# Opening of a two-layer transformer trunk: x loaded in two column halves, one mask made earlier

## The chip, the cores and the metric

One NeuronCore of a Trainium2 chip runs the whole program in one launch. The metric is the device time of that launch in microseconds (us). TensorE (PE) does matmuls and transposes, VectorE (DVE) and ScalarE (ACT) elementwise work, GpSimd (POOL) a few selects and rotary products, SyncE (SP) issues nearly all transfers from HBM (DMA).

## The reference, cut to what matters

```python
for l in range(2):
    h = rms_norm(x, norm1_g[l])                    # x: 256 tokens x 1024, float32
    z = h @ w_in[l] + b_in[l]                      # 1024 x 8448, cut into q/k/v, gMLP, dilated q/k/v, gates
    oa = sliding_window_attention(...)             # window 128, sinks, partial rotary
    ob = spatial_gating(...)                       # tril(w_spatial) inside chunks of 128
    oc = dilated attention, (window, dilation) in ((128, 1), (512, 4), (2048, 16))
    x = x + (sum of gated projections) @ w_out[l]
    x = x + hier_moe(rms_norm(x, norm2_g[l]), ...) # 32 experts
return rms_norm(x, norm_f_g)
```

## The kernel before, in words

Tokens lie on the 128 partitions in two blocks (`TB = 2`), so x is a tile `xs` of 128 x 2 x 1024. For `h @ w_in` the contraction must lie on partitions: x is turned on PE into 8 blocks of 128 columns (`KB = 8`), four of them per pair of PSUM banks. Each float32 product is made of three fp32r passes (high x high, low x high, high x low): ACT writes the rounded high part of a weight piece (`whi`, line 868) and of x (`ahi`, line 853), DVE the rest (`wlo`, line 1058; `alo`, line 1045). The gain of the norm goes in with `ahi` and `alo`; the norm's 1/rms comes in later, when a result leaves PSUM (`z_out`, line 1077).

The unit of the trunk is a half item, numbered j: two 128-row blocks of `w_in` by 512 columns, cast by one `whi` instruction and two `wlo` instructions (called here high(j), and low(j) with its first and second half), used by 12 matmuls of 512 columns on PE, called conv(j): `first_conv` for j = 0 to 3 in layer 0 and 1, `z_conv` afterwards. `whi` and `wlo` have two buffers, so high(j) waits until conv(j-2) is done. Weights come through a ring of four slots; a slot holds two half items.

The engines run written-out streams side by side and meet at semaphores. The opening in layer 0, by engine:

- SP issues x as one transfer (line 682), the first ring slot in two halves (line 679, for j = 0 and j = 1), three more slots (line 673), a broadcast of `b_in` (line 695), `w_spatial` (line 696), then slots as they come free; after four of these it waits for `masks_made` and stores the masks to DRAM (line 713), since their room is needed later.
- ACT issues the gains and the positions, loads a table, waits for `gains_done`, then does `x_high` (two blocks of x), high(0), `x_high`, high(1), four blocks of `x_high`, high(2), and so on; after high(3) it squares x for the norm (line 874).
- POOL makes index tiles and the identity; later it waits for `w_spatial` and masks its upper triangle (line 792).
- DVE makes the mask of branch A and the dilated mask 0 (lines 396, 399), waits for the turned gains and copies them (line 413), then follows ACT. A dilated mask with a step over 1 takes four instructions (lines 404, 405, 406, 399); masks 1 and 2 are made after low(4) and after low(7). After low(5) it evacuates the first results (line 1077), after low(6) it makes the rotary angles (`rope_angles`).
- PE runs `WARM_SETUP` = 7 float32 products of the identity with itself (two records each, line 1351), turns the gains (line 1355), waits for x and turns all 8 blocks (16 transposes, line 1363), then runs conv(0) on. Before conv(6) it turns `w_spatial` (line 1417).

Of the kernel before, what the change touches and what calls it, by code (L numbers as in the profile page):

```python
# [77 lines left out]
def trunk_program(nc, x, positions, norm1_g, w_in, b_in, attn_sinks, sgu_ln_g, sgu_ln_b, w_spatial,  # L78
# [7 lines left out]
    with ExitStack() as whole:  # L86
# [141 lines left out]
        y_low = sem("y_low")  # L228
        final_in = sem("final_in")
        masks_made = sem("masks_made")  # L230
        masks_out = sem("masks_out")
        masks_in = sem("masks_in")
        x_in = sem("x_in")
        pos_in = sem("pos_in")
        gain_in = sem("gain_in")
        gain2_in = sem("gain2_in")
# [111 lines left out]
            for _ in range(n):  # L348
                pe.matmul(ps[:, bank, 0:2 * P], ident[:], wr[:].rearrange("p k n -> p (k n)")[:, 0:2 * P], start=True, stop=True)

        WARM_SETUP, WARM_ROUTE, WARM_RANKS, WARM_LAST = 7, 7, 1, 1

        def load_sqrt_table(act):
            act.activation(warm[:], warm[:], ACT.Sqrt)
# [32 lines left out]
        def setup_dve(dve, link):  # L387
            dve.memset(warm[:], 1.0).then_inc(warm_set, 1)
            dve.wait_ge(consts_ready, 1)
            link(dve.tensor_copy(dist[:], dist_i[:]))  # L390
            link(dve.tensor_scalar(causal[:], dist[:], 0.0, None, ALU.is_ge))

            def make_mask(m, win, valid):

                if win < S - 1:
                    link(dve.scalar_tensor_tensor(out=within[:], in0=dist[:], scalar=float(win),
                                                  in1=valid[:], op0=ALU.is_le, op1=ALU.mult))
                    valid = within
                link(dve.tensor_scalar(m, valid[:], 1.0, -NEG, ALU.subtract, ALU.mult))

            def make_dilated(g, win, dil):

                if dil > 1:
                    link(dve.tensor_scalar(rem_i[:], dist_i[:], dil - 1, None, ALU.bitwise_and))
                    link(dve.tensor_copy(rem[:], rem_i[:]))
                    link(dve.scalar_tensor_tensor(out=rem[:], in0=rem[:], scalar=0.0, in1=causal[:],
                                                  op0=ALU.is_equal, op1=ALU.mult))
                make_mask(mask_c[:, g, :], win, rem if dil > 1 else causal)

            make_mask(mask_a[:], A_WIN - 1, causal)  # L410
            make_dilated(0, *C_PAIRS[0])
            dve.wait_ge(gains_ready, 1)
            dve.tensor_copy(gains[:, 0:DEPTH * KB], ps[:, 0, 0:DEPTH * KB]).then_inc(gains_done, 1)
            return make_dilated

        def rope_angles(dve, link):
# [172 lines left out]
        def trunk_stage(l):  # L589
            with ExitStack():  # L590
# [75 lines left out]
                with ExitStack():  # L666
                    @block.sync
                    def _(sp):
# [3 lines left out]
                            dst = ring[:, s, :].rearrange("p (k n) -> p k n", k=4)  # L672
                            sp.dma_start(dst, src).then_inc(ring_in[s], 16)

                        def load_first_item():
                            dst = ring[:, 0, :].rearrange("p (k n) -> p k n", k=4)
                            for half, landed in ((0, first_in), (1, ring_in[0])):
                                ks = slice(2 * half, 2 * half + 2)
                                sp.dma_start(dst[:, ks, :], w_in_l[:, ks, 0:BANK]).then_inc(landed, 16)

                        if l == 0:
                            sp.dma_start(xs[:], x.rearrange("o (t p) d -> p (o t) d", p=P)).then_inc(x_in, 16)
                        else:
                            sp.wait_ge(before_me.gu_ready, QUADS - 1)
                        load_first_item()
                        if l:
                            sp.wait_ge(before_me.y_ready, 2 * (QUADS - 1))
                            sp.wait_ge(before_me.st_ready, QUADS)
# [18 lines left out]
                        if l:  # L707
                            sp.wait_ge(before_me.gu_ready, QUADS)
                            sp.wait_ge(before_me.y_ready, 2 * QUADS)
                            sp.dma_start(masks, mask_store).then_inc(masks_in, 16)  # L710
                        else:
                            sp.wait_ge(masks_made, 1)
                            sp.dma_start(mask_store, masks).then_inc(masks_out, 16)
                        sp.dma_start(ln_gb[:, 0, :], sgu_ln_g[l].partition_broadcast(P)).then_inc(ln_in, 16)
                        sp.dma_start(ln_gb[:, 1, :], sgu_ln_b[l].partition_broadcast(P)).then_inc(ln_in, 16)
                        with sp.Fori(2, CHUNKS // 2) as it:
# [13 lines left out]
                        for i, (w, r) in enumerate(proj):  # L730
                            item = 34 + i
                            sp.wait_ge(low_split, 2 * (item - 4 + 1))
                            if w in ("a", "b", "out"):
                                dst = ring[:, item % 4, :].rearrange("p (k n) -> p k n", k=4)
                                for w_half, kb, n, nh, at in halved_blocks(w, r):
                                    src = w_half[kb * P:(kb + n) * P, nh * BANK:(nh + 1) * BANK].rearrange("(k p) n -> p k n", p=P)
                                    sp.dma_start(dst[:, at:at + n, :], src).then_inc(ring_in[item % 4], 16)
                            else:
                                src = w[2 * r * P:2 * (r + 1) * P, :].rearrange("(k p) n -> p k n", p=P)
                                dst = ring[:, item % 4, :].rearrange("p (k n) -> p k n", k=2)  # L740
                                sp.dma_start(dst, src).then_inc(ring_in[item % 4], 16)

                            if item == 35:
                                with nc.allow_non_contiguous_dma(reason="small parameters"):
                                    sp.dma_start(gain2[:], norm2_g[l].rearrange("(p k) -> p k", k=KB)).then_inc(ahead_in, 16)
                                    for w_r, first, n in ((w_router_group, 0, GROUPS), (w_router_expert, GROUPS, EXPERTS)):
                                        sp.dma_start(wr[:, :, first:first + n],
                                                     w_r[l].rearrange("(k p) n -> p k n", p=P)).then_inc(ahead_in, 16)
                            if item == 37:  # L750
                                sp.wait_ge(s_free, BATCHES)
                                if l == 0:
                                    sp.wait_ge(masks_out, 16)
                                load_last_down(sp, l, 3)
                            if item == 38:
                                sp.wait_ge(sv_ready, 1)
                                sp.wait_ge(pv_mm, turned_before(BATCHES))
                                load_ahead(18, 19)
                            if item == 39:
                                sp.wait_ge(obt_ready, 3)  # L760
                                sp.wait_ge(o_lo, 5)
                                load_ahead(0, 1, 5)
                            if item == 42:
                                sp.wait_ge(gated, 4)
                                load_ahead(2, 6)
                            if item == 43:
                                sp.wait_ge(gated, 8)
                                load_ahead(4)
# [268 lines left out]
                    def _(dve):  # L1037
# [43 lines left out]
                        for j in range(8):  # L1081
# [8 lines left out]
                            if l == 0 and j == 2:  # L1090
                                dve.wait_ge(gains_ready, 2)
                                dve.tensor_copy(gains[:, DEPTH * KB:], ps[:, 2, 0:DEPTH * KB]).then_inc(gains_done, 1)
                            if l == 0 and j in (4, 7):
                                make_dilated(1 if j == 4 else 2, *C_PAIRS[1 if j == 4 else 2])
                                if j == 7:
                                    dve.sem_inc(masks_made, 1)
                            if l and j == 2:
                                for q in range(4):
                                    dve.wait_ge(before_me.back_ready, 4 * (QUADS - 1) + q + 1)
# [114 lines left out]
                        low_at(43)  # L1214
                        dve.wait_ge(small_in, 32)
                        if l:
                            dve.wait_ge(masks_in, 16)
                        softmax_in(0)
                        low_at(44)
                        z_out(4, AHEAD - 1, BANK, AHEAD)  # L1220
# [125 lines left out]
                    def _(pe):  # L1346

                        if l == 0:
# [4 lines left out]
                            def turn_gains(i, bank):  # L1353
                                rows = DEPTH * KB
                                pe.transpose(ps[:, bank, 0:rows], gain_rows[:, i, :], ident[0:rows, 0:rows]).then_inc(gains_ready, 1)

                            pe.wait_ge(gain_in, 16)
                            turn_gains(0, 0)
                            pe.wait_ge(x_in, 16)
                            for k in range(KB):  # L1360
                                for tb in range(TB):
                                    at = (k % 2) * S + tb * P
                                    mm = pe.transpose(ps[:, 4 + k // 2, at:at + P], xs[:, tb, k * P:(k + 1) * P], ident[:])
                                if k % 2:
                                    mm.then_inc(turned, 1)
                            pe.wait_ge(gain2_in, 16)
                            turn_gains(1, 2)
                            pe.wait_ge(gains_done, 1)
# [52 lines left out]
                        for j in range(8):  # L1421
# [5 lines left out]
                            if j == 6:  # L1427
                                if l:
                                    pe.wait_ge(before_me.back_done, 4 * QUADS)
                                turn_w_spatial()  # L1430
                            if j < 4:
                                first_conv(j)
                            else:
# [946 lines left out]
```

## Time and profile before

| what | value |
|---|---|
| device time, 3 runs | median 1040.52 us (1038.24 to 1041.02) |
| profiled execution | 1039.62 us, span 1037.9 us |
| granted TensorE clock, mean over the span | 0.975 |
| PE / DVE / ACT / POOL busy | 956.8 / 576.1 / 426.5 / 58.5 us |
| DMA | 313.04 MB, mean 302 GB/s |

The span is what the profile covers, from the first instruction; the device time is some 1.7 us more. Busy time is a share over stages with different limits, so what matters for the change is the order of events in the first 40 us. A row of the timeline or the chain gives the start in us, the length in us, the engine, the line of the kernel and what it writes and reads; "x16" means 16 records merged.

### The profile page before, as it was taken

The page shows a single profiled execution, that of the slowest core. Times are in us where ns is not written, and L with a number is a line of the kernel's source. Part 1 is how long each engine was busy: PE and PEld are TensorE (multiplying, and loading weights), DVE is VectorE, ACT ScalarE, POOL GpSimd, SP SyncE. Part 2 cuts the span into 40 slices and gives each one's busy share as a digit, 9 for nine tenths or more (in the row PEclk, how much of TensorE's full clock was granted, in tenths as well). Part 3 has the DMA queues.
Part 4 walks back from the last instruction along what each step waited for, and adds up shares of the span by engine and source line. Part 5 has one row for each costly group of instructions (what it writes and reads, how often), then busy time and mean ns, then how long its engine had stood idle before and what let it go on. Part 6 is the DMA issues. An engine that isn't in the chain of part 4 may idle for free.

```text
span 1037.9 us, 15396 instructions
## 1 busy us (share of the span) xinstructions
PE 956.8 (92%) x5894; PEld 665.7 (64%) x5894; DVE 576.1 (56%) x1186; ACT 426.5 (41%) x907; POOL 58.5 (6%) x74
## 2 busy tenths in 40 slices
PE   8999999999999996795999999999999999875796
PEld 7788877777887432542588887777788954332343
DVE  7766788886873331121176668898869533222212
ACT  5434566666443210110354355666664431111122
POOL 1120400000010000000004004000000100000000
PEclk9999999999999997898999999999999999998889
DMA  9965533247999999999998655332589999999996
GB/s 347 357 222 186 198 123 122 82 122 260 397 360 381 418 426 424 420 423 427 414 380 278 202 187 177 122 122 82 167 291 369 381 402 417 426 422 424 425 424 255
DMA packets 97114, 313.04 MB, mean 302 GB/s; under 512 B 13424, under 2 KB 18576, under 8 KB 74512
## 3 DMA queue, kind: packets, MB, share of 16 engines
q1 hardware_dynamic: 96704, 312.04, 79.2%
q8 instruction: 45, 0.74, 0.3%
q14 instruction: 29, 0.24, 0.1%
q10 hardware_dynamic: 336, 0.02, 0.0%
HBM read 310.20 MB, written 1.84 MB: 301 GB/s over the span
## 4 chain that ended last, share of the span: by engine, by line
PE 67%; DMA 13%; DVE 7%; SPq 6%; ACT 3%; issue 2%; DVEq 0%; POOLq 0%; ACTq 0%
PE ps L1374 14%; PE ps L1376 13%; PE ps L1375 13%; DMA arena<-in_w_expert_up_dram 8%; SPq L479 6%; PE ps L1974 5%; DMA ring_rest<-in_w_expert_up_dram 5%; PE ps L2038 2%; PE ps L1949 2%; PE ps L1494 2%; PE ps L1399 2%; PE ps L1502 2%; DVE wlo L1058 2%; PE ps L2050 1%; PE ps L1922 1%
## 5 line engine op out<-in xcount | busy, mean ns | idle before, releaser
L1374 PE MATMUL ps<-whi,ahi 128*128 128x512 f32 (+1 forms) x736 | 285.0, 387 | 4.4 <-DVE wlo L1058 3.7
L1058 DVE TENSOR_TENSOR wlo<-arena,whi 128x512 fp32r<-128x512 f32 (+1 forms) x352 | 234.2, 704 | 91.3 <-ACT whi L868 88.8
L1376 PE MATMUL ps<-whi,alo 128*128 128x512 f32 (+1 forms) x736 | 277.1, 376 | 0.0
L1375 PE MATMUL ps<-wlo,ahi 128*128 128x512 f32 (+1 forms) x736 | 276.8, 376 | 0.0
L868 ACT CAST whi<-arena 128x1024 fp32r<-128x1024 f32 (+1 forms) x176 | 180.6, 1028 | 184.6 <-PE ps L1376 177.9
L1374 PEld LDWEIGHTS ps<-whi,ahi 128*128 128x128 f32 x736 | 138.5, 188 | 35.5 <-DVE wlo L1058 8.4
L1376 PEld LDWEIGHTS ps<-whi,alo 128*128 128x128 f32 x736 | 138.4, 188 | 26.0
L1375 PEld LDWEIGHTS ps<-wlo,ahi 128*128 128x128 f32 x736 | 138.7, 188 | 23.1
L1974 PE MATMUL ps<-arena,rows 128*32 128x512 f32 x416 | 92.1, 628 | 15.1 <-DMA arena<-in_w_expert_up_dram 11.6
L1974 PE MATMUL ps<-ring_rest,rows 128*32 128x512 f32 x352 | 78.0, 643 | 20.0 <-DMA arena<-in_w_expert_up_dram 17.0
L2166 DVE SCALAR_TENSOR_TENSOR acts<-ps,wslot,acts 128x256 f32<-128x256 f32 x16 | 7.7, 483 | 155.9 <-ACT acts L1884 132.8
L1884 ACT ACTIVATE acts<-ps,rslot 128x256 f32<-128x256 f32 x16 | 7.6, 474 | 156.2 <-PE ps L1974 153.3
L1949 PE MATMUL ps<-arena,work 128*128 128x128 f32 x448 | 55.5, 283 | 13.9 <-DVE arena L2125 12.2
L1949 PEld LDWEIGHTS ps<-arena,work 128*128 128x128 f32 x448 | 52.8, 197 | 24.0 <-DVE arena L2125 13.8
L948 ACT ACTIVATE probs<-probs,neg 128x128 f32<-128x128 f32 x112 | 49.5, 444 | 32.7 <-DVE neg L1183 32.7
L2050 PE MATMUL ps<-rows,st 128*128 128x512 f32 x112 | 54.9, 612 | 0.2
L2038 PE MATMUL ps<-arena,acts 128*32 128x512 f32 x288 | 48.1, 664 | 6.9 <-ACT acts L1888 4.9
L1974 PEld LDWEIGHTS ps<-ring_rest,rows 128*32 128x32 f32 x352 | 20.8, 117 | 52.4 <-issue 52.4
L1974 PEld LDWEIGHTS ps<-arena,rows 128*32 128x32 f32 x416 | 24.3, 115 | 44.6 <-issue 44.6
L2150 DVE TENSOR_TENSOR xs<-ps,xs 128x512 f32<-128x512 f32 x56 | 38.7, 691 | 22.7 <-PE ps L2050 22.7
L1077 DVE SCALAR_TENSOR_TENSOR arena<-ps,rstd,arena 128x512 f32<-128x512 f32 (+2 forms) x68 | 46.6, 726 | 2.2 <-PE ps L1376 2.2
L2142 DVE TENSOR_SCALAR rows<-ps,gain 128x128 f32<-128x128 f32 x56 | 15.8, 343 | 40.4 <-PE ps L1949 40.4
(282 smaller groups left out, 1043.2 us busy)
## 6 DMA issues: line engine op xcount, KB each, us to landing
arena<-in_w_in_dram SPq DMA_DIRECT2D x62, 1024.0 KB, 5.3
arena<-in_w_expert_down_dram SPq DMA_DIRECT2D x36, 1024.0 KB, 19.5
arena<-in_w_expert_gate_dram SPq DMA_DIRECT2D x34, 1024.0 KB, 25.6
arena<-in_w_expert_up_dram SPq DMA_DIRECT2D x34, 1024.0 KB, 26.0
ring_rest<-in_w_expert_down_dram SPq DMA_DIRECT2D x24, 1024.0 KB, 17.6
ring_rest<-in_w_expert_gate_dram SPq DMA_DIRECT2D x22, 1024.0 KB, 25.0
ring_rest<-in_w_expert_up_dram SPq DMA_DIRECT2D x22, 1024.0 KB, 26.1
arena<-in_w_proj_a_dram SPq DMA_DIRECT2D x8, 1024.0 KB, 5.0
```

What stands on the lines that cost most here:

```text
L479: sp.dma_start(slot, w[l, 4 * n + e].rearrange("(p k) f -> p (k f)", p=P)).then_inc(done, 16)
L868: act.copy(whi[:, jj % 2, 0:2 * w], half_slot(jj, w)).then_inc(hi_ready, 1)
L948: act.activation(probs[:, i, n, lo:hi], probs[:, i, n, lo:hi], ACT.Exp, bias=neg[:, i, tb, n:n + 1], accum_out=den[:, i, tb, n:n + 1])
L1058: dve.tensor_tensor(wlo[:, jj % 2, cols], half_slot(jj, w)[:, cols], whi[:, jj % 2, cols].bitcast(F32), ALU.subtract).then_inc(low_split i ...
L1077: dve.scalar_tensor_tensor(out=z[:, tb, cols], in0=ps[:, bank + tb, 0:w], scalar=rstd[:, tb:tb + 1], in1=z[:, 0, cols], op0=ALU.mult, op1= ...
L1374: pe.matmul(o, hi, rhs_hi, start=first, stop=False)
L1375: pe.matmul(o, hi, rhs_lo, start=False, stop=False)
L1376: return pe.matmul(o, lo, rhs_hi, start=False, stop=last)
L1949: mm = pe.matmul(ps[:, 4 + k // 4, (k % 4) * QUAD:(k % 4 + 1) * QUAD], work[:, tb, k * P:(k + 1) * P], onehot[:, n % 2, tb, :], start=(tb ...
L1974: mm = pe.matmul(ps[e * EC:(e + 1) * EC, n % 2, :].rearrange("p (a f) -> p a f", a=2), xsel[:, k, e * EC:(e + 1) * EC], w, start=(k == 0), ...
L2038: mm = pe.matmul(ps[e * EC:(e + 1) * EC, 2 + nh, :], at_sb[:, kf, e * EC:(e + 1) * EC], w, start=(kf == 0), stop=(kf == 1), skip_group_che ...
L2050: pe.matmul(ps[:, 4 + tb, :], st[:, n % 2, tb * P:(tb + 1) * P], y[:, nh * BANK:(nh + 1) * BANK], start=True, stop=True).then_inc(R.back_r ...
```

## The change: what it does

x is loaded in two column halves of 512 columns; the first half of the first ring slot is issued between them, the second half behind them. PE turns the first half of x (4 blocks) where it turned all of it, and the second half after conv(0), ahead of conv(1). Mask 1 is made right after the gains' copy in DVE's setup, mask 2 after low(4), and none after low(7). Two warming products fewer run on PE. One semaphore does the work of two around the masks' trip through DRAM.

```diff
-        masks_out = sem("masks_out")
-        masks_in = sem("masks_in")
+        masks_moved = sem("masks_moved")
         x_in = sem("x_in")
+        x_rest_in = sem("x_rest_in")
...
-        WARM_SETUP, WARM_ROUTE, WARM_RANKS, WARM_LAST = 7, 7, 1, 1
+        WARM_SETUP, WARM_ROUTE, WARM_RANKS, WARM_LAST = 5, 7, 1, 1
...
             dve.tensor_copy(gains[:, 0:DEPTH * KB], ps[:, 0, 0:DEPTH * KB]).then_inc(gains_done, 1)
+            make_dilated(1, *C_PAIRS[1])
...
+                        def load_x_columns(half, landed):
+                            cols = slice(half * BANK, (half + 1) * BANK)
+                            sp.dma_start(xs[:, :, cols], x.rearrange("o (t p) d -> p (o t) d", p=P)[:, :, cols]).then_inc(landed, 16)
+
                         if l == 0:
-                            sp.dma_start(xs[:], x.rearrange("o (t p) d -> p (o t) d", p=P)).then_inc(x_in, 16)
+                            load_x_columns(0, x_in)
                         else:
                             sp.wait_ge(before_me.gu_ready, QUADS - 1)
-                        load_first_item()
+                        load_first_item(0, first_in)
+                        if l == 0:
+                            load_x_columns(1, x_rest_in)
+                        load_first_item(1, ring_in[0])
...
-                            if l == 0 and j in (4, 7):
-                                make_dilated(1 if j == 4 else 2, *C_PAIRS[1 if j == 4 else 2])
-                                if j == 7:
-                                    dve.sem_inc(masks_made, 1)
+                            if l == 0 and j == 4:
+                                make_dilated(2, *C_PAIRS[2])
+                                dve.sem_inc(masks_made, 1)
...
+                            def turn_x_columns(half):
+                                pe.wait_ge(x_rest_in if half else x_in, 16)
+                                for k in range(4 * half, 4 * half + 4):
+                                    for tb in range(TB):
+                                        at = (k % 2) * S + tb * P
+                                        mm = pe.transpose(ps[:, 4 + k // 2, at:at + P], xs[:, tb, k * P:(k + 1) * P], ident[:])
+                                    if k % 2:
+                                        mm.then_inc(turned, 1)
+
                             pe.wait_ge(gain_in, 16)
                             turn_gains(0, 0)
-                            pe.wait_ge(x_in, 16)
-                            for k in range(KB):
-                                for tb in range(TB):
-                                    at = (k % 2) * S + tb * P
-                                    mm = pe.transpose(ps[:, 4 + k // 2, at:at + P], xs[:, tb, k * P:(k + 1) * P], ident[:])
-                                if k % 2:
-                                    mm.then_inc(turned, 1)
+                            turn_x_columns(0)
...
+                            if l == 0 and j == 1:
+                                turn_x_columns(1)
                             if j < 4:
                                 first_conv(j)
```

## Rows read from the trace of the kernel before

**Rows 1.** The page: shares of the chain of waits, by engine.
```profile
PE 67%; DMA 13%; DVE 7%; SPq 6%; ACT 3%; issue 2%; DVEq 0%; POOLq 0%; ACTq 0%
```

**Rows 2.** Chain of waits, first 42 us: start, length, what the end waited for.
```profile
0.82 5.24 DMA xs<-in_x_dram
...
8.73 5.72 PE ps L1399 x24
...
14.53 1.05 ACT whi L868
...
19.01 1.29 DVE wlo L1058 x2
...
22.60 2.03 DVE wlo L1058
...
33.80 0.50 PE ps L1374
```

**Rows 3.** Issues of the first 2.2 us: line, count, KB, us to landing.
```profile
gain_rows<-in_norm_g_dram ACTq DMA_DIRECT2D x1, 8.0 KB, 3.2
arena<-in_w_in_dram SPq DMA_DIRECT2D x1, 512.0 KB, 6.2
arena<-in_w_in_dram SPq DMA_DIRECT2D x1, 512.0 KB, 7.6
```

**Rows 4.** Timeline of the first 8 us, by engine.
```profile
0.81 0.95 ACTq L880 DMA_DIRECT2D gain_rows<-in_norm_g_dram  x2
...
1.30 0.98 SPq L679 DMA_DIRECT2D arena<-in_w_in_dram  x2
...
2.08 3.36 PE L1351 MATMUL ps<-ident 128*128 128x128 f32 x14 [2.08 <-POOL ident L378]
...
5.71 0.17 DVE L413 COPY gains<-ps 128x16 f32<-128x16 f32 x1 [1.50 <-PE ps L1355]
...
6.10 1.97 PE L1363 MATMUL ps<-ident,xs 128*128 128x128 f32 x16 [0.49 <-DMA xs<-in_x_dram]
6.86 0.84 ACT L853 ACTIVATE ahi<-ps,gains 128x256 fp32r<-128x256 f32 x2 [3.04 <-PE ps L1363]
7.59 1.04 ACT L868 CAST whi<-arena 128x1024 fp32r<-128x1024 f32 x1
```

**Rows 5.** Weight loads by line: duration ns min/median/max, first and last start.
```profile
L1351 PEld LDWEIGHTS ps<-ident x14: 288/333/338, 2.1 to 4.8; 128*128 128x128 f32 x14
...
L1363 PEld LDWEIGHTS ps<-ident,xs x16: 138/141/144, 6.1 to 7.7; 128*128 128x128 f32 x16
```

**Rows 6.** Timeline: DVE and POOL at 20 to 24 us and at 125 us.
```profile
20.22 0.35 DVE L404 TENSOR_SCALAR rem_i<-dist_i 128x384 int32<-128x384 int32 x1
...
21.99 2.64 DVE L1058 TENSOR_TENSOR wlo<-arena,whi 128x512 fp32r<-128x512 f32 x2
22.25 1.84 POOL L792 TENSOR_SCALAR_AFFINE_SELECT probs<-probs 128x1536 f32<-128x1536 f32 x1 [19.26 <-DMA probs<-in_w_spatial_dram]
...
124.66 0.93 POOL L808 TENSOR_TENSOR arena<-arena,mixed 128x192 f32<-128x192 f32 x1
125.06 1.40 DVE L1077 SCALAR_TENSOR_TENSOR arena<-ps,rstd,arena 128x512 f32<-128x512 f32 x2
```

**Rows 7.** Timeline from 31 to 35 us: ACT, SP and PE.
```profile
31.13 1.07 ACT L868 CAST whi<-arena 128x1024 fp32r<-128x1024 f32 x1
...
33.01 5.91 SPq L713 DMA_DIRECT2D mask_store<-spare_slot  x1
...
33.15 0.39 PE L1376 MATMUL ps<-whi,alo 128*128 128x512 f32 x1
```

**Rows 8.** Stretches in layer 0's experts: PE busy, granted clock, DMA share, GB/s.
```profile
394.00:396.00 2.00, 1.43 (x16) 1.00 0.98 410
396.00:398.00 2.00, 0.50 (x2) 0.98 1.05 438
...
404.00:406.00 2.00, 2.00 (x14) 0.81 1.03 430
```

More of the change, by code:

```diff
@@ L673, in load_z_item, with load_first_item @@
                             sp.dma_start(dst, src).then_inc(ring_in[s], 16)
-                        def load_first_item():
+                        def load_first_item(half, landed):
                             dst = ring[:, 0, :].rearrange("p (k n) -> p k n", k=4)
-                            for half, landed in ((0, first_in), (1, ring_in[0])):
-                                ks = slice(2 * half, 2 * half + 2)
-                                sp.dma_start(dst[:, ks, :], w_in_l[:, ks, 0:BANK]).then_inc(landed, 16)
+                            ks = slice(2 * half, 2 * half + 2)
+                            sp.dma_start(dst[:, ks, :], w_in_l[:, ks, 0:BANK]).then_inc(landed, 16)
+                        def load_x_columns(half, landed):
+                            cols = slice(half * BANK, (half + 1) * BANK)
+                            sp.dma_start(xs[:, :, cols], x.rearrange("o (t p) d -> p (o t) d", p=P)[:, :, cols]).then_inc(landed, 16)
                         if l == 0:
-                            sp.dma_start(xs[:], x.rearrange("o (t p) d -> p (o t) d", p=P)).then_inc(x_in, 16)
+                            load_x_columns(0, x_in)
                         else:
                             sp.wait_ge(before_me.gu_ready, QUADS - 1)
-                        load_first_item()
+                        load_first_item(0, first_in)
+                        if l == 0:
+                            load_x_columns(1, x_rest_in)
+                        load_first_item(1, ring_in[0])
                         if l:
@@ L709, in _ @@
                             sp.wait_ge(before_me.y_ready, 2 * QUADS)
-                            sp.dma_start(masks, mask_store).then_inc(masks_in, 16)
+                            sp.dma_start(masks, mask_store).then_inc(masks_moved, 16)
                         else:
                             sp.wait_ge(masks_made, 1)
-                            sp.dma_start(mask_store, masks).then_inc(masks_out, 16)
+                            sp.dma_start(mask_store, masks).then_inc(masks_moved, 16)
                         sp.dma_start(ln_gb[:, 0, :], sgu_ln_g[l].partition_broadcast(P)).then_inc(ln_in, 16)
@@ L752, in _ @@
                                 if l == 0:
-                                    sp.wait_ge(masks_out, 16)
+                                    sp.wait_ge(masks_moved, 16)
                                 load_last_down(sp, l, 3)
@@ L1216, in _ @@
                         if l:
-                            dve.wait_ge(masks_in, 16)
+                            dve.wait_ge(masks_moved, 32)
                         softmax_in(0)
```

## The prediction

> **What bounds the kernel now.** First the page: PE is busy for 956.8 us of the 1037.9 (the table of the profile) and holds 67% of the chain of waits, DMA 13% [rows 1]. So time taken out of the opening reaches the end only if PE starts its unbroken run earlier; every later load is released by work that moves along with it. Then the chain of the first 42 us [rows 2], read for who holds PE up. Until 8.73 it is x (issued 0.82, landed 6.06) and what must happen to it. From 8.73 PE works without a break to 14.45. Then the chain goes through ACT and DVE: high(3) at 14.53, the squares, low(4) at 19.01, mask 1 from 20.22 [rows 6], low(5) with a second half that takes 2.03 where the two of low(4) take 1.29 together, the rotary angles, mask 2, low(8). It comes back to PE at 33.80 with conv(8), and from there PE rows follow each other at 0.23 us. What the change is worth is therefore how much earlier conv(8) starts, not how much earlier conv(0) does.
>
> **Part by part.**
>
> *Warming products, 7 to 5.* 14 records take 3.36 us, 0.24 each [rows 4]; four fewer free 0.96 us, so they end at 4.48. The first gains were issued at 0.81 and took 3.2 us [rows 3, 4]: landed at 4.0, covered. Their turn moves to 4.5 and DVE's copy from 5.71 to about 4.85, ending at 5.0. Without this cut the copy would end at 5.88 and be what ACT waits for.
>
> *Half of x first.* All of x lands at 6.06. The 512 KB behind it, issued at 1.30, landed 6.2 later, at 7.50 [rows 3, 4]: 1.44 us for half a megabyte. The first half of x should land 1.44 before 6.06, at 4.6. Bounds: 0 earlier (if the halves are served side by side) and 2.6 earlier (half of 5.24). I take 4.7, near the row. The rest keeps its bytes and order: the first weight half lands at about 6.1, the second half of x at 7.5; the last of the four transfers stays at its 9.4, since the same bytes are ahead of it. SP issues one transfer more, 0.48 us, which its queue covers (its fifth issue waits for room anyway).
>
> *From the landing to conv(0).* Before: x at 6.06, first pair turned and `ahi` started at 6.86, conv(0) at 8.73 [rows 2, 4]. So 0.80 from landing to ACT, and 1.87 from ACT's start to PE (two `ahi`, one `whi`). After: 4.7 + 0.80 + 1.87 = 7.4. But the clock: the warming products load weights in 333 ns, the turns of x in 141 [rows 5], so the former ran at the lower level (1.2 GHz) though the granted column shows 1.00, and the higher one (2.4 GHz) came only after the last of them had begun at 5.0. Turns that start at 4.75 will partly run at the lower level: up to four at 0.24 instead of 0.12, at most 0.5 more. conv(0) then starts between 7.4 and 7.9, which is 0.8 to 1.3 earlier. ACT needs the gains (5.0) and the first weights (6.1, needed at 6.3): both cover.
>
> *Mask 1 in the setup.* Four instructions, from 20.22 until low(5) at 21.99 before [rows 6]: 1.77. Now from 5.0 to 6.8 on a DVE that had nothing until 7.73. It is due at `alo` for the first pair, which needs ACT's two `ahi`, at 6.4 to 6.8. If the cover is gone the price is 0.3 at most, and PE first uses `alo` 0.9 after conv(0) starts, so zero.
>
> *The second half's turns on PE.* 8 of 16, half of 1.97: 0.98 us. Before, they lay beside ACT's work. Now PE's order puts them between conv(0) and conv(1), in the open. The 0.8 to 1.3 gained shrinks to between -0.2 and +0.3 at conv(1). Behind them wait conv(1) and ACT's four `ahi`; high(2) would end near 13.6, conv(2) begins at 13.9, so it is only just covered. I take a lead of 0.15, and write it s.
>
> *Up to low(5).* high(3) follows the end of conv(1), and squares, high(4), low(4) and then a mask follow high(3), so s is carried. Mask 2 now stands where mask 1 stood, same four instructions, 1.77. Then comes a fixed post. POOL's select runs from 22.25 to 24.09, released by the landing of `w_spatial`, which has the same bytes ahead of it as before [rows 6]. DVE's second half of low(5), started at 22.60, does not end before 24.63 [rows 2]. With s = 0.15 it starts at 22.45, still behind 22.25, and ends at 24.63 again. s is lost there: 0.
>
> The Trainium skill, GPSIMD Engine Reference, section Specifications, says that POOL shares its SBUF interfaces with VectorE, with contention for DVE instructions in a two-port mode or with two SBUF inputs. `wlo` has two SBUF inputs and was held, while `z_out`, with one input in PSUM, took 1.40 for two beside POOL [rows 6], so the trace agrees; by the rule the two-input step of a mask would be held as well, which matters for a rival below.
>
> *No mask after low(7).* The 1.77 us of mask 2 ahead of low(8) on DVE go. What is late next: high(8) on ACT, 31.13 plus 1.05, so 32.2 [rows 7]; low(8)'s first half then ends at 32.9. PE's last matmul of conv(7) starts at 33.15, the next can start 0.23 later at 33.38, and now does; before it was 33.80 [rows 2, 7]. That is 0.42, plus 0.11 because a matmul behind a gap takes 0.50 rather than 0.39: 0.53. Bounds: 0 (if a load or ACT is late instead) and 0.53, as PE has no gap left to close. SP reached the store of the masks at 33.01 behind other issues [rows 7], when they had just been made, so an earlier mask doesn't move it or what queues behind.
>
> *Sum against the profiled execution:* 1039.62 - 0 (opening, lost at POOL's select) - 0.53 = 1039.1. That execution lies 0.9 under the median of the three runs; against the median it would be 1040.0. The mean of the four times shown is 1039.85, and 1039.85 - 0.53 = 1039.3, which I predict.
>
> **The rivals.**
>
> *A. The lead is large enough to slip past POOL's select.* The second half of low(5) escapes if it starts before 22.25, so from s = 0.35 on; the upper end of my own estimate is 0.3, and a landing of `w_spatial` 0.2 later would do the rest. Then it ends near 22.9 instead of 24.63, and `z_out`, not held by POOL, follows. DVE is 1.7 us earlier up to low(7), where conv(7) takes over as the limit. With the 0.42 at conv(8) the gain is about 2.1: 1037.7. For it: x's half could land at 4.6 or earlier. Against: the lower clock in the first turns.
>
> *B. PE loses its higher clock in the opening: slower.* After the change PE has work to 4.5, a few turns to about 5.9, then a gap to 7.4 or more, while before it had 7 products to 5.4 and gaps of 0.5. In the experts' stage the clock fell at the end of four microseconds in which PE was busy for 1.93 (394 to 398), and came back only in the stretch 404 to 406 [rows 8]. Had the opening's clock stayed low, then as in the opening before (lower level from 2.08 to past 5.0) some 3.3 us of conv(0) and conv(1) would run at half speed: 1.65 lost, where the lead was 0.15 less the slower turns. low(4) is 1.7 late, mask 2 falls under POOL's select (22.25 to 24.09) and is held, low(5) ends near 26.7 instead of 24.63, 2.1 late; less the 0.53, 1.6 slower: 1041.4. It decides from any low stretch of more than about 1 us in conv(0) or conv(1). The Trainium skill, TensorE: Matmul & The Clock Gate, section on the HAM clock gate, says that the throttled state is the default and activity lifts it; rows 5 and 8 agree, and it speaks against cutting warming work.
>
> *C. Nothing moves.* conv(8) waits for something else (high(8) later, as ACT is held by the rotary functions), 1039.85. For it: ACT's row at 31.13 leaves 0.5 us of room only.
>
> **How the numbers follow.** Forecast 0.45, A 0.25, B 0.18, C 0.12. A measurement can tell about 0.3% from no change, 3.1 us, and no case but an extreme one reaches that: faster than 1037.4 only if A comes with a low draw of the runs (they spread over 2.8 us), 0.13; slower than 1043.6 only if B's low clock lasts as long as at 398 to 405, 0.04; within, 0.83. The forecast's own range is 1038.2 to 1040.6, the spread of the runs moved by 0.5. For 8 in 10 I add most of A and B: 1037.0 to 1041.7.
>
> **What would show it.** Right: the first turn of x near 4.8; the gains' copy near 4.9; mask 1 over by 6.9 with no wait on ACT from it; conv(0) at 7.4 to 7.9; 8 turns ahead of conv(1), which starts at 11.2 to 11.7; the second half of low(5) again near 2 us long, ending at 24.6; no gap ahead of conv(8), its first matmul near 33.4. Wrong: a 0.65 us second half of low(5) (A); weight loads over 300 ns or matmuls 0.43 apart behind 7.4 (B); a gap ahead of conv(8) that ACT or a load ends (C); x's first half landing near 6, which would undo the first three steps at once.

## The result and the profile after

The changed kernel is slower: median 1044.37 us (1043.24 to 1045.10, 6 runs) against 1040.68 (1038.24 to 1041.47, 6 runs), ratio 1.0036 with a 95% interval of 1.0024 to 1.0048. Run again later beside its variants it gave 1.0018 (1.0010 to 1.0027). Both lie above 1; how much above, 1.9 or 3.7 us, the two comparisons don't agree on (their intervals just overlap); 2 to 4 us is what can be said.

The chain of waits of the changed kernel, first 27 us (start, length, what the end waited for), answers to [rows 2]:

```profile
0.82 4.47 DMA xs<-in_x_dram
5.33 1.97 PE ps L1368 x8
7.52 0.91 issue
8.43 4.32 PE ps L1408 x12
12.74 0.87 PE ps L1368 x8
13.62 2.78 PE ps L1408 x12
16.48 1.05 ACT whi L875
...
20.96 1.29 DVE wlo L1065 x2
...
22.56 1.74 DVE rem L405
...
26.18 0.50 PE ps L1383
```

```profile
2.08 2.21 PEld L1357 LDWEIGHTS ps<-ident 128*128 128x128 f32 x10 [2.08 <-POOL ident L378]
4.51 0.18 PEld L1361 LDWEIGHTS ps<-ident,gain_rows 16*128 16x128 f32 x1 [0.22 <-issue]
5.33 1.57 PEld L1368 LDWEIGHTS ps<-ident,xs 128*128 128x128 f32 x8 [0.64 <-DMA xs<-in_x_dram]
7.23 0.18 PEld L1361 LDWEIGHTS ps<-ident,gain_rows 16*128 16x128 f32 x1 [0.33 <-issue]
8.39 1.36 PEld L1408 LDWEIGHTS ps<-whi,ahi 128*128 128x128 f32 x4 [0.98 <-issue]
9.85 1.53 PEld L1408 LDWEIGHTS ps<-whi,alo 128*128 128x128 f32 x4
11.43 0.89 PEld L1408 LDWEIGHTS ps<-wlo,ahi 128*128 128x128 f32 x4
```

The rise falls between the row at 9.85 and the row at 11.43. The gains' weight load is the handiest gauge: 0.18 at the lower level, 0.13 at the higher. In the kernel before it read 0.13 already at 5.37:

```profile
5.37 0.13 PEld L1355 LDWEIGHTS ps<-ident,gain_rows 16*128 16x128 f32 x1 [0.22 <-issue]
```

From conv(0)'s first matmul to the work behind it on PE it is 4.16 us here and 2.82 before, so the level cost 1.34 there. What follows from a late conv(1) is on VectorE of the changed kernel, timeline from 20 us, which answers to [rows 6]:

```profile
22.17 0.36 DVE L404 TENSOR_SCALAR rem_i<-dist_i 128x384 int32<-128x384 int32 x1
22.56 1.73 DVE L405 CAST rem<-rem_i 128x384 f32<-128x384 int32 x1
...
25.44 1.29 DVE L1065 TENSOR_TENSOR wlo<-arena,whi 128x512 fp32r<-128x512 f32 x2 [0.16 <-DVE spare_slot L399]
26.65 1.41 DVE L1084 SCALAR_TENSOR_TENSOR arena<-ps,rstd,arena 128x512 f32<-128x512 f32 x2
```

And on POOL in the same kernel:

```profile
22.53 1.55 POOL L799 TENSOR_SCALAR_AFFINE_SELECT probs<-probs 128x1536 f32<-128x1536 f32 x1 [19.54 <-DMA probs<-in_w_spatial_dram]
```

The cast of mask 2 meets POOL's select and takes 1.73 instead of 0.36. low(5) ends at 26.7 where it ended at 24.63, PE waits 1.41 us for its first half, conv(5) starts at 26.18 (22.74 before), and conv(8) at 35.84 where it was 33.80: 2.0 us late, with no gap ahead of it. Both traces then run in parallel to the router of layer 0, and part again in its experts' stage. Chain of waits of the changed kernel:

```profile
313.06 1.71 PE ps L585 x16
...
511.61 3.71 PE ps L2007 x64
```

The same two places in the kernel before:

```profile
311.11 1.71 PE ps L584 x16
...
508.13 3.68 PE ps L1996 x64
```

1.95 late at the router, 3.48 late after the experts, and 3.7 late at the end of the span (1041.6 against 1037.9). The extra 1.5 us is one of the questions below.

### The profile page after: what moved, and what is told of

It is laid out like the page before. It is cut to its first block, busy times and chain, and to the rows that moved or that the text cites. A ratio compares the mean times of both kernels' runs of the same rounds, so it can differ in the third digit from the quotient of the medians.

```text
span 1041.6 us, 15389 instructions
## 1 busy us (share of the span) xinstructions
PE 961.9 (92%) x5890; PEld 670.1 (64%) x5890; DVE 576.1 (55%) x1186; ACT 426.6 (41%) x907; POOL 57.9 (6%) x74
## 4 chain that ended last, share of the span: by engine, by line
PE 63%; DMA 15%; SPq 10%; DVE 7%; ACT 4%; issue 2%; DVEq 0%; ACTq 0%
PE ps L1383 14%; PE ps L1385 13%; PE ps L1384 13%; DMA arena<-in_w_expert_up_dram 10%; SPq L480 10%; DMA ring_rest<-in_w_expert_up_dram 5%; PE ps L1985 4%; PE ps L1505 2%; PE ps L1513 2%; PE ps L1408 1%; PE ps L1960 1%; PE ps L2049 1%; PE ps L1933 1%; ACT probs L955 1%; DVE wlo L1065 1%
## 5 line engine op out<-in xcount | busy, mean ns | idle before, releaser
L1985 PE MATMUL ps<-arena,rows 128*32 128x512 f32 x416 | 95.5, 641 | 12.5 <-DMA arena<-in_w_expert_up_dram 10.2
L1985 PE MATMUL ps<-ring_rest,rows 128*32 128x512 f32 x352 | 81.4, 670 | 21.6 <-DMA arena<-in_w_expert_up_dram 17.5
L1960 PEld LDWEIGHTS ps<-arena,work 128*128 128x128 f32 x448 | 56.0, 207 | 23.2 <-DVE arena L2136 13.9
L1960 PE MATMUL ps<-arena,work 128*128 128x128 f32 x448 | 58.8, 294 | 13.1 <-DVE arena L2136 12.2
L2049 PE MATMUL ps<-arena,acts 128*32 128x512 f32 x288 | 45.1, 617 | 6.1 <-ACT acts L1899 6.1
```

Source lines behind the costliest of these rows:

```text
L1960: mm = pe.matmul(ps[:, 4 + k // 4, (k % 4) * QUAD:(k % 4 + 1) * QUAD], work[:, tb, k * P:(k + 1) * P], onehot[:, n % 2, tb, :], start=(tb ...
L1985: mm = pe.matmul(ps[e * EC:(e + 1) * EC, n % 2, :].rearrange("p (a f) -> p a f", a=2), xsel[:, k, e * EC:(e + 1) * EC], w, start=(k == 0), ...
L2049: mm = pe.matmul(ps[e * EC:(e + 1) * EC, 2 + nh, :], at_sb[:, kf, e * EC:(e + 1) * EC], w, start=(kf == 0), stop=(kf == 1), skip_group_che ...
```

## The experiments

Each kernel was timed against the kernel before on the same chip as itself; not all were on one chip, so two variants are compared through their ratios. "Products" are the warming products; "2 +" stands for two ahead of them on another tile, "+ 4" and "+ 3" for some behind them. The columns conv(0) and conv(8) give the start of the first matmul in the one trace of each kernel. "Level rises" is where that trace's first clock record begins; the weight loads agree with it in each. "Experts" is the distance of the two rows just shown, router to end of layer 0's experts. All but the ratio is one execution each.

| kernel | products | ratio (95% interval) | conv(0) | level rises | conv(8) | experts |
|---|---|---|---|---|---|---|
| before | 7 | | 8.73 | 5.4 | 33.80 | 197.0 |
| changed | 5 | 1.0036 (1.0024, 1.0048) | 8.43 | 11.3 | 35.84 | 198.6 |
| after_again | 5 | 1.0018 (1.0010, 1.0027) | 8.47 | 14.4 | 37.27 | 198.8 |
| a_warm7 | 7 | 0.9993 (0.9983, 1.0003) | 8.67 | 7.8 | 34.81 | 198.7 |
| a_fill | 5 + 4 | 0.9991 (0.9982, 0.9999) | 8.86 | 7.5 | 34.70 | 198.7 |
| a_warm0 | 0 | 1.0015 (1.0006, 1.0025) | 8.48 | 13.1 | 36.70 | 196.4 |
| a_early | 2 + 5 | 1.0012 (1.0001, 1.0023) | 8.59 | 14.2 | 37.23 | 197.1 |
| a_both_masks | 5 | 1.0008 (0.9997, 1.0020) | 8.56 | 14.4 | 37.05 | 198.0 |
| a_halves | 7 | 1.0006 (0.9997, 1.0014) | 8.49 | 6.2 | 34.34 | 197.8 |
| b_warm5 | 5 | 1.0004 (0.9994, 1.0014) | 10.03 | 12.2 | 36.04 | 197.9 |
| b_masks | 7 | 0.9993 (0.9982, 1.0005) | 9.13 | 5.9 | 33.92 | 196.7 |
| b_delay2 | 7 | 1.0014 (1.0004, 1.0024) | 10.15 | 10.0 | 36.82, of which 1.7 inserted | 197.9 |
| b_early | 2 + 7 | 0.9995 (0.9986, 1.0004) | 10.30 | 10.2 | 35.28 | 197.1 |
| b_both_masks | 7 | 0.9986 (0.9977, 0.9994) | 9.27 | 5.1 | 32.70 | 197.5 |
| b_both_fill | 7 + 3 | 0.9976 (0.9966, 0.9987) | 9.21 | 6.7 | 32.65 | 197.0 |

**a_warm7.** In the changed kernel:

```diff
-        WARM_SETUP, WARM_ROUTE, WARM_RANKS, WARM_LAST = 5, 7, 1, 1
+        WARM_SETUP, WARM_ROUTE, WARM_RANKS, WARM_LAST = 7, 7, 1, 1
```

> The changed kernel with 7 warming products instead of 5, all else as changed. Theory of the clock (PE stayed at its lower clock until about 11.6 us because the warming products ended at 4.6 instead of 5.4): turns of x at the higher level (weight loads near 141 ns, not over 300), conv(0) at 0.23 us per matmul, conv(8) near 33.8 to 34.2 us instead of 35.8, total 1040 to 1041, 3 to 4 us under the changed kernel's 1044.4. Rival of the order (the 8 turns between conv(0) and conv(1) and mask 2 under GpSimd's select cost it, whatever the clock): clock high but conv(8) still at 35 or later, total 1043 or more.

Measured 0.9993: 2.6 us below the changed kernel's 1.0018 of a comparison of the same size, from two products; the two intervals don't meet. conv(8) at 34.81 is later than the 33.8 to 34.2 of the clock theory. In this trace the first turns of x still ran at the lower level, conv(0) did not; conv(1) starts at 12.31 (11.55 before), and the last step of mask 2 meets POOL's select and takes 1.75:

```profile
7.48 0.18 PEld L1361 LDWEIGHTS ps<-ident,gain_rows 16*128 16x128 f32 x1 [0.33 <-issue]
8.64 0.76 PEld L1408 LDWEIGHTS ps<-whi,ahi 128*128 128x128 f32 x4 [0.98 <-issue]
...
22.49 1.75 DVE L399 TENSOR_SCALAR spare_slot<-rem 128x384 f32<-128x384 f32 x1
```

So the warming products carry the loss, and the order of the turns does not carry most of it.

**b_warm5.** The same edit the other way in the kernel before (7 to 5).

> The kernel before with 5 warming products instead of 7, nothing else. Theory of the clock: PE has work from 2.08 to 4.6 and from 6.1 on; the lower level lasts into conv(0), conv(8) comes 1.5 to 2.5 us later than 33.8, total 1042 to 1044. Rival of the order: the turns of x lie under ACT's work here anyway and two warming products are covered, so conv(8) at 33.8 and total as before, 1040.5.

The trace does what the clock theory says (level up at 12.2 us, conv(8) at 36.04), but the median of the runs hardly moves: 1.0004 (0.9994 to 1.0014), where 1042 to 1044 us were expected. So in the kernel before the same cut costs nothing that can be told from none, and at most 1.5 us. The table offers a reason: with 7 products the level rises at 5.4 us in one execution and at 10.0 in another (b_delay2 has the same opening), and the latter would have begun conv(8) near 35.1, only 0.9 ahead of b_warm5. If many executions open like that, the median of the kernel before already holds late openings. How many do is not shown, with one trace of each kernel. The weight loads of b_delay2, still low through all 16 turns:

```profile
6.38 3.28 PEld L1363 LDWEIGHTS ps<-ident,xs 128*128 128x128 f32 x16 [0.83 <-DMA xs<-in_x_dram]
9.99 0.14 PEld L1355 LDWEIGHTS ps<-ident,gain_rows 16*128 16x128 f32 x1 [0.33 <-issue]
```

**b_masks.** In the kernel before, with `make_dilated(1, ...)` behind the gains' copy, and

```diff
-                            if l == 0 and j in (4, 7):
+                            if l == 0 and j == 4:
```

making mask 2 there.

> The kernel before with only the masks moved (mask 1 after the gains' copy, mask 2 after low(4), none after low(7)). Both theories: no gap ahead of conv(8), which starts at 33.4 instead of 33.8; mask 1 done at 7.7, just before the first alo. Total 0.5 us less than before, within what can be measured. A third view, that mask 1 in the setup holds ACT or PE in the opening, would show conv(0) later than 8.9.

0.9993 fits the half microsecond but can't tell it from nothing. The trace fits: conv(0) 0.40 late with x, which landed 0.4 later here, conv(8) only 0.12 late.

**b_delay2.** In the kernel before:

```diff
                                 z_conv(j, 2, BANK, j + 1)
+                                if l == 0 and j == 7:
+                                    for _ in range(8):
+                                        pe.matmul(ps[:, 7, 0:P], ident[:], ident[:], start=True, stop=True)
```

> The kernel before with 8 further products of the identity with itself on PE right after conv(7) of layer 0 (about 2.0 us at the higher clock), result unused. It asks what a 2 us delay at conv(8) costs at the end, since the changed kernel's trace is 2.0 us late there and 3.7 late at the end. If a delay is carried one to one: total 2 us more, 1042.5. If the load-bound experts' stage makes more of it: 3.5 to 4 us more, 1044 to 1044.5, with the extra arising between 370 and 395 us. If slack behind swallows it: under 1 us.

1.0014, so 1.5 us (0.4 to 2.5). In the trace the products stand from 35.12 to the start of conv(8) at 36.82, 1.7 us. That fits one to one; a doubling in the load-bound stage (3.5 to 4 us) is ruled out. The last column of the table says the same: the experts' stage takes 196.4 to 198.8 us, whatever the opening was; a_warm0, with a late opening, has the shortest. The changed kernel's further 1.5 us in the first trace lies within what executions differ by there, and needs no cause in the change; which of these executions is usual is not shown.

**after_again.** The changed kernel unaltered.

> The changed kernel itself, unaltered, on the same chip and in as many runs as its variants. Theory of the clock: in its opening TensorE reaches the higher level only at 9 to 12 us, conv(8) at 35 to 36, total 2.5 to 4 us over the kernel before. If the first comparison drew an unlucky set of openings (in four variants the rise came at 5.4, 6.4, about 8 and 10 us with the same 7 products), the median here is only 0.5 to 1.5 us over the kernel before.

1.0018, between the two expectations. Its level rose even later, at 14.4 us.

**a_halves.** The changed kernel with 7 products and the masks in their old places, so the halves of x alone.

> The kernel before with the halves of x alone: the two-part load and the second half's turns between conv(0) and conv(1), with 7 warming products and the masks in their old places. Theory of the clock: not faster and not slower than before by more than 1 us, since the earlier conv(0) is eaten by the 8 turns in the open; conv(1) at 12.3 us, 0.7 later than in the kernel before, conv(8) 0.5 to 1.2 later. Rival of the order: the turns in the open alone give most of the 3.7 us.

1.0006 (0.9997 to 1.0014): nothing that can be told from no change, though this trace had the higher level ahead of conv(0). conv(1) began at 12.11, where it began at 11.55 before.

**b_both_masks.** In the kernel before:

```diff
+            make_dilated(1, *C_PAIRS[1])
             dve.wait_ge(gains_ready, 1)
             dve.tensor_copy(gains[:, 0:DEPTH * KB], ps[:, 0, 0:DEPTH * KB]).then_inc(gains_done, 1)
+            make_dilated(2, *C_PAIRS[2])
+            dve.sem_inc(masks_made, 1)
...
-                            if l == 0 and j in (4, 7):
-                                make_dilated(1 if j == 4 else 2, *C_PAIRS[1 if j == 4 else 2])
-                                if j == 7:
-                                    dve.sem_inc(masks_made, 1)
```

> The kernel before with both dilated masks in VectorE's setup: mask 1 ahead of the wait for the gains, where VectorE sits idle for 1.5 us, mask 2 behind the gains' copy; no mask after low(4) or low(7). Nothing else. If mask 2 after low(4) and its meeting with GpSimd's select hold conv(5), the gap ahead of conv(5)'s first or second half goes (0.3 to 1.4 us in all traces so far), conv(8) comes 1.5 to 2.1 earlier than with the mask there, total 1.5 to 2 us under before. If the 1.77 us behind the gains' copy only shift the wait to alo and conv(0), less than 0.5.

0.9986: about 1.5 us faster, as expected at the low end. conv(8) is at 32.70, and low(5) runs its natural 1.30 with POOL's select beside it, because its second half starts before the select does:

```profile
21.57 1.30 DVE L1061 TENSOR_TENSOR wlo<-arena,whi 128x512 fp32r<-128x512 f32 x2 [0.74 <-ACT whi L871]
22.79 1.40 DVE L1080 SCALAR_TENSOR_TENSOR arena<-ps,rstd,arena 128x512 f32<-128x512 f32 x2
```

and POOL beside it:

```profile
22.64 1.63 POOL L795 TENSOR_SCALAR_AFFINE_SELECT probs<-probs 128x1536 f32<-128x1536 f32 x1 [19.66 <-DMA probs<-in_w_spatial_dram]
```

This is rival A's escape from the select, reached by taking the mask out rather than by a lead.

**b_early.** In the kernel before, VectorE fills `wst[:, 0, :]` first of all, and PE runs two products on it ahead of the wait for the identity.

> The kernel before with two warming products more, run on a tile that VectorE fills at 0.9 us, so that PE works from about 1.2 us instead of 2.1. Theory of the clock: the higher level is reached ahead of the turns of x (weight loads near 141 ns) in more executions, conv(8) no later than 33.8, and the median falls by 0.5 to 1.5 us and the spread of the runs (5 us over 35 runs of the kernel before) narrows. Rival: the opening's clock has nothing to do with the spread, which arises in the load-bound stages: median and spread as before.

0.9995, not told from 1. The trace had PE at work from 1.13 and the level still low until 10.2: starting earlier did not bring the rise forward in this execution.

**a_warm0.** The changed kernel with `WARM_SETUP` 0.

> The changed kernel with no warming product at all (0 instead of 5). In the three traces with 5 products the higher level came only at 11.5 to 14 us. If 5 products buy nothing (all or nothing, decided by what PE does without a break up to about 5.4 us), the time is that of the changed kernel, 1.5 to 2.5 us over the kernel before, and the level rises at 10 to 15 us. If each product adds its share, this is 1.5 to 2.5 us slower than the changed kernel.

1.0015, as with 5 (1.0018). Five products buy nothing that can be measured; seven buy 2.6 us.

**a_early.** The changed kernel with two products ahead on the filled tile, as in b_early.

> The changed kernel with two products ahead of its 5, on a tile that VectorE fills at 0.9 us, so PE works from 1.1 to 4.6 us. Theory that the length of unbroken work decides: 3.4 us of it, as with 7 products, gives the changed kernel with 7 products back (0.5 us under the kernel before), the higher level at times before the turns of x. Rival, that work must last until past 5 us, whatever its start: as the changed kernel, 1.5 to 2.5 us over.

1.0012, the rival's side. PE worked from 1.13 to 4.6, as long as seven products do, and the level rose at 14.2 us:

```profile
1.13 0.93 PEld L1358 LDWEIGHTS ps<-wst 128*128 128x128 f32 x4 [1.13 <-DVE warm L389]
2.08 2.21 PEld L1361 LDWEIGHTS ps<-ident 128*128 128x128 f32 x10
...
5.50 1.57 PEld L1372 LDWEIGHTS ps<-ident,xs 128*128 128x128 f32 x8 [0.80 <-DMA xs<-in_x_dram]
...
13.42 0.22 PEld L1372 LDWEIGHTS ps<-ident,xs 128*128 128x128 f32 x1
13.85 0.97 PEld L1372 LDWEIGHTS ps<-ident,xs 128*128 128x128 f32 x7 [0.20 <-issue]
```

Against a_warm7 the seven products lie about 0.9 us earlier: they end at 4.6, with a gap before x. Which of the two, the early end or the gap, keeps the level down is not told apart here.

**a_fill.** In the changed kernel:

```diff
                             turn_gains(0, 0)
+                            for _ in range(2):
+                                pe.matmul(ps[:, 3, 0:P], ident[:], ident[:], start=True, stop=True)
                             turn_x_columns(0)
                             pe.wait_ge(gain2_in, 16)
                             turn_gains(1, 2)
+                            for _ in range(2):
+                                pe.matmul(ps[:, 3, 0:P], ident[:], ident[:], start=True, stop=True)
```

> The changed kernel with its 5 warming products, and two further products behind the turn of the gains (in the gap ahead of x) and two behind the turn of the second gains (in the gap ahead of conv(0)), so that PE has hardly a gap between 2.1 us and conv(0). Theory of the clock: the higher level no later than conv(0)'s first matmuls in its trace, total 2 to 3 us under the changed kernel, so at or 1 us under the kernel before. Rival (the order of the turns costs it): no gain, 1.5 to 2.5 us over before.

0.9991: 2.8 us below the changed kernel, though its conv(0) starts 0.4 later. The second gains' load is at the higher level at 7.6, where the changed kernel's read 0.18 at 7.2:

```profile
7.60 0.14 PEld L1361 LDWEIGHTS ps<-ident,gain_rows 16*128 16x128 f32 x1 [0.26 <-issue]
```

This is the cleanest test: four products that compute nothing, put in PE's gaps, give back the loss. The first products end at 4.6 here as in the changed kernel and the gains are turned at the same time, so an earlier end of the products does no harm by itself.

**b_both_fill.** b_both_masks with two products behind the first turn of gains and one behind the second.

> The kernel before with both dilated masks in the setup (which was 1.8 us faster), 7 warming products, and two more behind the turn of the gains and one behind that of the second gains. Theory of the clock: the higher level in more executions ahead of the turns of x, another 0.3 to 1 us, total 2.2 to 2.8 us under the kernel before. If the products only stand in PE's way in executions that are at the lower level, no gain over the 1.8.

0.9976: 2.5 us under the kernel before, 1.0 under b_both_masks (their intervals overlap, so the 1.0 is likely but not shown). PE works without a gap from 9.21; the chain of waits:

```profile
9.21 11.14 PE ps L1402 x48
20.35 0.45 PE ps L1377
```

This version beats both kernels.

**a_both_masks.** The changed kernel with b_both_masks' edit.

> The changed kernel (halves of x, 5 warming products) with both dilated masks in VectorE's setup, so that no mask stands between low(4) and low(5), where in the changed kernel's traces it meets GpSimd's select and one of its steps takes 1.7 us instead of 0.36. If the low clock costs only through that meeting (a late low(4), then mask 2, then the select), conv(5) follows conv(4) without its 1.4 us gap, conv(8) comes about 3 us earlier than the changed kernel's, total at or under the kernel before although the clock rises late. If the low clock's own loss reaches the end by itself, 1 us or more over before remains.

1.0008 (0.9997 to 1.0020), and conv(8) at 37.05 all the same. With the level low until 14 us low(4) itself came at 22.5, under POOL's select, and four `wlo` steps took 3.86 where they take 2.6:

```profile
22.52 3.86 DVE L1067 TENSOR_TENSOR wlo<-arena,whi 128x512 fp32r<-128x512 f32 x4 [0.38 <-ACT whi L877]
26.30 1.40 DVE L1086 SCALAR_TENSOR_TENSOR arena<-ps,rstd,arena 128x512 f32<-128x512 f32 x2
```

So taking the mask out only moved the meeting: the select now holds low(4), and conv(4) starts late instead of conv(5). In this trace the low level's own delay (conv(1) at 14.9 instead of 11.55) reaches conv(8) without the mask. The median does not settle how much of the loss is the level alone: it lies between the kernel before and the changed one, and apart from neither.

## Why the prediction was wrong

It forecast 0.5 us faster and gave the case that happened, rival B, 0.18. Step by step:

- *Half of x first* was mis-sized: landed at 5.29, 0.77 before the whole x of the trace before, not 1.4. In the traces with the whole x it landed at 6.1 to 6.6, so against those the gain is 0.8 to 1.3. Its price was read from how far apart x and the transfer behind it landed (1.44).
- *Warming products, 7 to 5* is the step that failed. It was taken as 0.96 us freed at no cost. The rows had shown that the higher level came only after the last product had begun at 5.0 [rows 5], which was read as "the turns may partly run at the lower level, 0.5 more". With the products ending near 4.6 instead, ahead of the gap before x, the level did not rise until 11.3 to 14.4 us, in every trace where they ended there or earlier and the gap stayed open (six of six); in the other nine it rose at 5.1 to 10.2. The pair that the prediction read the levels from, 333 against 141 ns, sets a product beside a turn. Like with like it is 333 against 192 for a product and 231 against 141 for a turn, and the conclusion holds.
- *From the landing to conv(0)* held within that: 5.29 + 1.26 (slow turns) + 1.88 = 8.43. The lead was 0.30, not 0.8 to 1.3.
- *The second half's turns on PE* cost 0.8 to 1.0 in the open, as said. Together: -0.30 (lead), +1.34 (conv(0) 4.16 instead of 2.82), +0.79 (turns) put conv(1) at 13.38, 1.83 late.
- *Up to low(5)*: the sum had s = +0.15; it was -1.95 (low(4) at 20.96). Then rival B's course: mask 2 under the select and held, low(5) ending at 26.7 as written. B had the second half of low(5) and the way to low(8) set the time behind it; in the trace the first half of low(5) did, and PE had no gap from 26.18 on.
- *No mask after low(7)* was right: no gap ahead of conv(8).
- The price. Rival B was worked out at 1.6 us slower; conv(8) came 2.0 late in its trace, and the medians say 1.9 and 3.7. The 2.0 is the difference to the best opening of the kernel before. That an execution of the kernel before can itself open late does not show in its one trace.
- The forecast's own range, 1038.2 to 1040.6, is not what its words give: the four times it names, 1038.24 to 1041.02, moved by 0.5 are 1037.7 to 1040.5. The measured median lies above both.

The chance is where the judgement failed. The Trainium skill, TensorE: Matmul & The Clock Gate, section on the HAM clock gate, says the throttled state is the default and activity lifts it. The prediction cited it as speaking against the cut and still treated the rise as given, at about the same time as before. The traces agree with the page as to the default: the level was low at the start of all fifteen. More work did not always lift it sooner, though: with no product it rose at 13.1, with seven ending at 4.6 at 14.2.

## What to carry to other kernels

Warm-up work on TensorE whose result nobody uses can still pay, by when the clock rises: cut it only with its effect on weight-load times in hand. In this opening, filling the gaps up to the first real matmul paid and starting the work earlier did not. Time gained by an earlier load is worth only what the next fixed post leaves of it, and here the order of a mask against another engine's select was worth more than the load. A single trace of an opening shows one execution out of several kinds; trust what repeats over traces.

## What was not expected of the hardware

- The rise of the level varies between executions of the same opening: with 7 products and PE busy from 2.08, it came at 5.4 in one trace (the kernel before) and at 10.0 in another (b_delay2). That may be part of the 5 us over which 35 runs of the kernel before lie (1038.6 to 1043.6); no run shows how much.
- Equal lengths of work are not equal: 3.4 us of products ending at 5.4 gave a rise between 5.1 and 10.0 us, 3.4 us ending at 4.6 (a_early) one at 14.2.
- The granted clock column read 1.00 in stretches where weight loads took 333 ns instead of 192 (products) and 231 instead of 141 (turns). It knows the fall in the experts' stage (0.50 at 398 to 404 in the kernel before); at the start of a trace, ahead of the first clock record, the durations tell the level and not the column.
- POOL's select held a cast of VectorE (1.73 instead of 0.36) and a scalar step of a mask (1.75 instead of 0.36 in a_warm7), not only steps with two SBUF inputs; a step with an input in PSUM was not held (1.40 for two of `z_out` beside the select in b_both_masks, as without it). A step that had begun ahead of the select kept its time too (low(5) there).
